# Modulation matmuls four units at a time in four column strips, and a wait moved to the evacuation of v

## What is computed

```python
mod = silu(c) @ w_ada + b_ada          # (9, 6*1024): 8 sample sequences and the prompt
shift1, scale1, gate1, shift2, scale2, gate2 = split(mod)
h = rmsnorm(x) * (1 + scale1) + shift1
q, k, v, conv..., gates... = h @ w_in  # w_in is (1024, 5120)
s = q @ k.T * HEAD_DIM ** -0.5 + rel_bias[:, rel]   # relative bias, then softmax, @ v
# then convolution, mixing, x += gate1 * mix, norm 2, routing, 32 experts, final norm
```

## Time and profile before

| | us |
|---|---|
| median of 3 runs | 1923.19 (1922.13 to 1927.28) |
| span of the profiled execution | 1918.4 |
| TensorE busy | 1676.0 (87%) |
| VectorE busy | 962.2 (50%) |
| ScalarE busy | 766.2 (40%) |
| POOL busy | 216.4 (11%) |

### The profile page before, as it was taken

The page is one execution under the profiler, slowest core; times in us unless marked ns, Lnnn a source line. Parts: engine busy times, 40 slices in busy tenths (PEclk is TensorE's granted clock), DMA queues, the critical chain, the costliest instruction groups (busy, mean ns, idle before and its releaser), DMA issues.

```text
span 1918.4 us, 22477 instructions
## 1 busy us (share of the span) xinstructions
PE 1676.0 (87%) x8467; PEld 1388.9 (72%) x8467; DVE 962.2 (50%) x1156; ACT 766.2 (40%) x869; POOL 216.4 (11%) x336
## 2 busy tenths in 40 slices
PE   6984999999989989999998994499999999999930
PEld 1244987886449989999997883377777777777720
DVE  0451102554320272222223545488888888888847
ACT  0221123663112022111121322077777777777734
POOL 2004401110000000000000002100000000000036
PEclk9997999999999999999998997699999999999965
DMA  9857512003421111211225333299999999999963
GB/s 344 284 84 219 191 64 71 1 2 113 157 68 54 44 34 31 83 50 50 58 71 199 121 99 110 92 398 398 396 396 395 395 394 394 396 391 393 342 220 142
DMA packets 194747, 371.34 MB, mean 194 GB/s; under 512 B 10699, under 2 KB 69107, under 8 KB 194546
## 3 DMA queue, kind: packets, MB, share of 16 engines
q1 hardware_dynamic: 170784, 289.92, 42.1%
q0 software_dynamic: 18976, 62.93, 10.2%
q10 hardware_dynamic: 4914, 17.49, 2.3%
HBM read 324.49 MB, written 47.89 MB: 194 GB/s over the span
## 4 chain that ended last, share of the span: by engine, by line
PE 74%; DVE 10%; ACT 6%; issue 3%; DMA 2%; another core or an unknown queue 2%; ACTq 1%; POOL 0%; SPq 0%; POOLq 0%; DVEq 0%; PEldq 0%
PE ps L1565 19%; PE ps L1567 18%; PE ps L1566 18%; PE ps L1548 4%; DVE mlo L1084 4%; ACT mhi L938 3%; PE ps L1692 3%; PE ps L1673 2%; ACT yy L958 2%; PE ps L1755 2%; PE ps L1732 2%; PE ps L1879 2%; PE ps L1682 1%; DMA bada<-in_b_ada_dram 1%
## 5 line engine op out<-in xcount | busy, mean ns | idle before, releaser
L1084 DVE TENSOR_TENSOR mlo<-mraw,mhi 128x2048 fp32r<-128x2048 f32 x188 | 420.5, 2288 | 38.9 <-ACT mhi L938 38.7
L938 ACT CAST mhi<-mraw 128x2048 fp32r<-128x2048 f32 x192 | 357.2, 1910 | 27.3 <-DMA mraw<-in_w_e_down_dram 27.2
L1565 PE MATMUL ps<-hTh,ring_r 128*128 128x384 f32 x864 | 291.2, 337 | 39.5 <-DVE ring_r L1084 31.6
L1567 PE MATMUL ps<-hTh,ring_r 128*128 128x384 f32 x864 | 290.6, 336 | 0.0
L1566 PE MATMUL ps<-hTl,ring_r 128*128 128x384 f32 x864 | 290.6, 336 | 0.0
L1565 PE MATMUL ps<-mhi,xTh 128*128 128x512 f32 x512 | 207.5, 405 | 22.0 <-DVE mlo L1084 19.6
L1566 PE MATMUL ps<-mlo,xTh 128*128 128x512 f32 x512 | 201.7, 394 | 0.0
L1567 PE MATMUL ps<-mhi,xTl 128*128 128x512 f32 x512 | 201.5, 394 | 0.0
L1565 PEld LDWEIGHTS ps<-hTh,ring_r 128*128 128x128 f32 x864 | 163.8, 190 | 41.2 <-DVE ring_r L1084 29.8
L1084 DVE TENSOR_TENSOR ring_r<-ring_f,ring_r 128x1024 fp32r<-128x1024 f32 x56 | 68.2, 1224 | 199.9 <-ACT ring_r L748 199.5
L1567 PEld LDWEIGHTS ps<-hTh,ring_r 128*128 128x128 f32 x864 | 163.6, 189 | 0.0
(11 more groups left out here) (302 smaller groups left out, 2549.4 us busy)
## 6 DMA issues: line engine op xcount, KB each, us to landing
mraw<-in_w_e_gate_dram SPq DMA_DIRECT2D x64, 1024.0 KB
mraw<-in_w_e_up_dram SPq DMA_DIRECT2D x64, 1024.0 KB
mraw<-in_w_e_down_dram SPq DMA_DIRECT2D x64, 1024.0 KB, 7.9
aring<-in_w_ada_dram SPq DMA_DIRECT2D x24, 1024.0 KB
ring_f<-in_w_in_dram SPq DMA_DIRECT2D x80, 256.0 KB, 4.5
y_d<-yy ACTq DMA_DIRECT2D x32, 512.0 KB, 6.8
y_d<-zrow POOLq DMA_DIRECT2D x68, 128.0 KB, 4.0
kc<-in_cache_attn_k_dram SPq DMA_DIRECT2D x8, 1024.0 KB, 5.3
```

The costliest lines, as they stand in the source:

```text
L938: nc.scalar.copy(mhi[j][:], mraw[j][:]).then_inc(s["gu_hi" if j < 4 else "d_hi"], 1)
L1084: V.tensor_tensor(out, value, high.bitcast(F32), ALU.subtract).then_inc(sig, 1)
L1565: mm(out, xh, wh, start=start, stop=False)
L1567: return mm(out, xl, wh, start=False, stop=stop)
```

## The change

The 12 units become three groups of four. `modulations(a)` runs the matmuls of a group slice by slice, the four units in turn; unit g of a group has its result in PSUM partitions 32g to 32g + 8 of one bank, so each uses its own strip of 32 columns of the array. `modc`, `bada` and `spread` get the same four strips of partitions. The ring for `w_ada` gets eight places: group 0 lies where `hTh` and `hTl` come later, groups 1 and 2 share the four old places. SP issues groups 0 and 1 at the start and group 2 when `unit_used` is 8. On TensorE group 0 comes first, then four spreads, group 1 ahead of the transposes of tile 3, group 2 after norm 1. The first six `w_in` units all wait for `unit_used` 12, and the first two chunks of q leave norm 1 and stand in `project` with the third. ScalarE's wait for `rel_out` moves to before the evacuation of v, its waits for `mod_out` go away, and POOL builds `spread` in four strips.

```diff
--- before.py
+++ after.py
@@ -164,7 +164,8 @@
 
-        aring = [at(f"aring{j}", [P, KT, 512], RING + j * SLOT if j < 3 else A(108)) for j in range(4)]
+        aring = [[at(f"aring{b}{j}", [P, KT, 512], A(16 * j) if b == 0 else RING + j * SLOT if j < 3 else A(108))
+                  for j in range(4)] for b in range(2)]
         hTh = at("hTh", [P, KT, T], A(0), F32R)
...
@@ -318,6 +319,9 @@
 
+        def ada_in(a, g):
+            return s["ada_mid"] if a == 1 else landed[g]
+
 
@@ -329,6 +333,11 @@
         NADA = 6 * D // 512
+        AG = NADA // 4
+
+        def strip(g):
+            return slice(32 * g, 32 * g + SEQS + 1)
+
         ada_units = [cols(w_ada2, c, 512) for c in range(NADA)]
...
@@ -397,22 +403,26 @@
 
-            for u, halves in enumerate(ada_units):
-                wait(sp, s["unit_used"], u - 3)
-                for i, src in enumerate(halves):
-                    sp.dma_start(aring[u % 4][:, 4 * i:4 * i + 4, :], src).then_inc(landed[u % 4], 16)
-                wait(sp, s["mod_sb"], u - 2)
-                sp.dma_start(bada[:, u % 3, :],
-                             bass.AP(b_ada.tensor, b_ada.offset + u * 512, [[0, SEQS + 1], [1, 512]])
-                             ).then_inc(landed[u % 4], 16)
+            for a in range(AG):
+                if a == 2:
+                    sp.wait_ge(s["unit_used"], 8)
+                for g in range(4):
+                    u = 4 * a + g
+                    sp.dma_start(bada[strip(g), a, :],
+                                 bass.AP(b_ada.tensor, b_ada.offset + u * 512, [[0, SEQS + 1], [1, 512]])
+                                 ).then_inc(ada_in(a, g), 16)
+                for i in range(2):
+                    for g in range(4):
+                        sp.dma_start(aring[min(a, 1)][g][:, 4 * i:4 * i + 4, :], ada_units[4 * a + g][i]
+                                     ).then_inc(ada_in(a, g), 16)
+
             def mixture(t):
                 wait(sp, s["o_done"], t - 1)
                 sp.dma_start(mix_parts(t)[1], mix_d[t]).then_inc(s[f"mix_in{t % 2}"], 16)
 
             for u, halves in enumerate(units):
                 if u == UK + 2:
-                    for r in range(3):
-                        sp.wait_ge(s[f"mod_out{r}"], MOD_OUT[r])
+                    sp.wait_ge(s["mod_out"], 16 * (NADA - 4))
                     sp.dma_start(modrep_d.rearrange("(q t) c -> q t c", t=DEC),
@@ -427,7 +437,7 @@
                 if u < NSLOT:
-                    sp.wait_ge(s["unit_used"], min(9 + u, NADA))
+                    sp.wait_ge(s["unit_used"], NADA)
                 elif u < NU - 2:
@@ -522,13 +532,15 @@
             link(nc.gpsimd.memset(spread[:], 1.0))
-            link(nc.gpsimd.affine_select(out=spread[:, 0, :], in_=spread[:, 0, :], compare_op=ALU.is_ge, fill=0.0,
-                                         base=-SEQROW, pattern=[[0, P]], channel_multiplier=1))
-            link(nc.gpsimd.affine_select(out=spread[:, 1, :], in_=spread[:, 1, :], compare_op=ALU.is_ge, fill=0.0,
-                                         base=0, pattern=[[1, P]], channel_multiplier=-DEC))
-            nc.gpsimd.affine_select(out=spread[:, 1, :], in_=spread[:, 1, :], compare_op=ALU.is_ge, fill=0.0,
-                                    base=DEC - 1, pattern=[[-1, P]], channel_multiplier=DEC
-                                    ).then_inc(s["consts"], 1)
+            for g in range(4):
+                own = spread[strip(g)]
+                link(nc.gpsimd.affine_select(out=own[:, 0, :], in_=own[:, 0, :], compare_op=ALU.is_ge, fill=0.0,
+                                             base=-SEQROW, pattern=[[0, P]], channel_multiplier=1))
+                link(nc.gpsimd.affine_select(out=own[:, 1, :], in_=own[:, 1, :], compare_op=ALU.is_ge, fill=0.0,
+                                             base=0, pattern=[[1, P]], channel_multiplier=-DEC))
+                link(nc.gpsimd.affine_select(out=own[:, 1, :], in_=own[:, 1, :], compare_op=ALU.is_ge, fill=0.0,
+                                             base=DEC - 1, pattern=[[-1, P]], channel_multiplier=DEC))
+            pool.sem_inc(s["consts"], 1)
             link(nc.gpsimd.memset(before[:], 1.0))
...
@@ -729,14 +740,13 @@
                 act.wait_ge(s["mod_sb"], u + 1)
-                act.dma_start(mod_d[:, u * 512:(u + 1) * 512], modc[:, u % 3, :]
-                              ).then_inc(s[f"mod_out{u % 3}"], 16)
+                act.dma_start(mod_d[:, u * 512:(u + 1) * 512], modc[strip(u % 4), u // 4, :]
+                              ).then_inc(s["mod_out"], 16)
 
             for u in range(2):
                 act.wait_ge(s["bc_ps"], u + 1)
                 for side in range(2):
                     nc.scalar.copy(shift1[:, side, u * 512:(u + 1) * 512], bank(6 + side)).then_inc(s["bc_sb"], 1)
-            modulation_out(4)
             act.wait_ge(s["consts"], 3)
@@ -765,18 +775,14 @@
                 b = 2 * (t % 2)
-                if t == 5:
-                    weights_high_to(1)
                 nc.scalar.copy(hTh[:, :, t * P:(t + 1) * P], bank(b, 2).rearrange("p (k c) -> p k c", k=KT)
                                ).then_inc(s["n1_evac"], 1)
-                if LEAD + t < NADA:
-                    modulation_out(LEAD + t)
+                if t in (4, 5, 6, 7):
+                    modulation_out(t)
 
             weights_high_to(2)
-            act.wait_ge(s["rel_out"], 16)
-
-            for r in range(3):
-                act.wait_ge(s[f"mod_out{r}"], MOD_OUT[r])
+            for u in range(8, NADA):
+                modulation_out(u)
             g = 0
@@ -799,6 +805,7 @@
                 g += 1
+            act.wait_ge(s["rel_out"], 16)
             for t in range(NT):
@@ -1048,12 +1055,9 @@
             def modulation(u):
-                dve.wait_ge(s["unit_used"], u + 1)
-                if u >= 7:
-                    dve.wait_ge(s[f"mod_out{u % 3}"], 16 * len(range(4 + (u - 4) % 3, u, 3)))
-                elif u >= 3:
-                    dve.wait_ge(s["bc_ps"], min(u - 2, 4))
-                V.tensor_tensor(modc[:, u % 3, :], ps[0:SEQS + 1, 4 + u % 2, :], bada[:, u % 3, :],
+                a, g = u // 4, u % 4
+                dve.wait_ge(s["unit_used"], 4 * a + 4)
+                V.tensor_tensor(modc[strip(g), a, :], ps[strip(g), 4 + a % 2, :], bada[strip(g), a, :],
                                 ALU.add).then_inc(s["mod_sb"], 1)
@@ -1065,9 +1069,6 @@
             V.tensor_copy(relrow[:, 4 * P:], bass.AP(relin, n, [[NREL, H], [-1, n]])).then_inc(s["rel_sb"], 1)
-
-            modulation(4)
-
 
@@ -1104,13 +1105,13 @@
                 V.tensor_tensor(ht[:, r, :], ht[:, r, :], shift1[:, side, :], ALU.add).then_inc(s["n1_h"], 1)
-                if LEAD + t < NADA:
-                    modulation(LEAD + t)
+                if t in (4, 5, 6, 7):
+                    modulation(t)
                 if t >= 1:
                     rows_rest(t - 1)
-                if t == 6:
-                    weights_rest_to(1)
             rows_rest(NT - 1)
+            for u in range(8, NADA):
+                modulation(u)
 
@@ -1541,13 +1542,15 @@
 
-            def modulation(u):
-                pe.wait_ge(landed[u % 4], 48 * (u // 4 + 1))
-                wait(pe, s["mod_sb"], u - 1)
+            def modulations(a):
+                wait(pe, s["mod_sb"], 4 * (a - 1))
+                for g in range(4):
+                    pe.wait_ge(ada_in(a, g), (48, 4 * 48, 96)[a])
                 for k in range(KT):
-                    last = mm(ps[0:n, 4 + u % 2, :], cT[:, k, :], aring[u % 4][:, k, :],
-                              start=(k == 0), stop=(k == KT - 1))
-                last.then_inc(s["unit_used"], 1)
+                    for g in range(4):
+                        last = mm(ps[strip(g), 4 + a % 2, :], cT[:, k, :], aring[min(a, 1)][g][:, k, :],
+                                  start=(k == 0), stop=(k == KT - 1))
+                last.then_inc(s["unit_used"], 4)
 
@@ -1592,8 +1595,7 @@
                         done += len(parts(c0, cn)) if split else 1
-                        if u0 > 0 or m > 0 or c == len(TOKCH) - 1:
-                            chunk_of(u0 + m, c, owner, base_count + done)
+                        chunk_of(u0 + m, c, owner, base_count + done)
                         if c0 == 0:
@@ -1606,27 +1608,23 @@
                 for side in range(2):
-                    last = mm(ps[:, 6 + side, :], spread[:, side, :], modc[:, u % 3, :], start=True, stop=True)
+                    last = mm(ps[:, 6 + side, :], spread[strip(u), side, :], modc[strip(u), 0, :],
+                              start=True, stop=True)
                 last.then_inc(s["bc_ps"], 1)
 
-            for u in range(LEAD + 1):
-                modulation(u)
-                if 1 <= u <= 4:
-                    spread_rows(u - 1)
+            modulations(0)
+            for u in range(4):
+                spread_rows(u)
             for t in range(NT):
                 r = t % 2
```

(25 more changed lines are left out.)

## The result

The changed kernel took 1945.95 us (median of four runs, 1945.16 to 1947.43), the kernel before 1924.38 (four runs, 1922.13 to 1927.28). The ratio is 1.0126, 95% interval 1.0112 to 1.0139. The medians lie 21.6 us apart, the ratio makes it 24. Forecast were 1941 and "slower". The profiled execution spans 1945.8 us, 27.4 more than the one of before (1918.4).

The account below looks back on a forecast made before the run. Loads sharing eight DMA engines with the bias table were taken to hold TensorE before 192 us. Group 2, weights and q's units put unit 1's end at 200.6, 17.6 later: 1918.4 to 1936.0, plus 4.8, about 1941; range 1932 to 1985.

Parts of the forecast that it names:

- Who held the hole of before: TensorE's 33 us wait near 133 us: weight unit 1's late landing beside the bias table's DMA, not the `rel_out` semaphore.
- One packet per turn on eight engines: DMA queues: eight engines serve one weight packet per table packet of 0.94 us, 64 turns for the table.
- Strips at 0.43 us per four: Modulation matmuls: four strips run together, so a group takes 6.9 us, plus 1.6 after idleness.
- Group 0: First four modulation units: data lands at about 34.5 us, matmuls run from 34.7 to 43.2.
- Spread and scale: Between group 0 and norm 1: 12.7 us from 43.2, with hops ending at 56.7; 7 us gained for norm 1.
- Norm 1, group 1, group 2, weights: Norm 1 3.8 us per tile; group 1 67.1 to 75.6; group 2 159.6 to 168.1; weights' first matmul at 174.
- Unit 0 of q: All three chunks now follow group 2 and take 14.1 us, to 188.1; unit 1 adds 12.5, to 200.6.
- Sum: q's unit 1 ends at 200.6 instead of 183.0, 17.6 us later; profiled span 1936.0, median 1940.8, say 1941.
- By parts: Summary of the loss: data 16 us later, unit 0 12.5 later, the stall as long as before.
- The moved wait: ScalarE's wait for `rel_out`, moved from before q to before v, never ended last, so gives nothing.
- Strips without overlap: Rival (a): a group's matmuls run serially, 27.5 us (cold 29.1); +60.7 us, about 1984; chance 0.18.
- a group 2 that passes the table: Rival (b), the second: engines serve many 2 KB packets per table packet, group 2 lands at 100 to 101; about 1881; chance 0.07.

Follow-up runs that it names:

- the wait-only run: Kernel before with one edit, ScalarE's wait for `rel_out` moved from ahead of q's evacuation to ahead of v's: 1921.03 us beside 1921.69, ratio 0.9999.
- the two-step table: Kernel before with the bias table written once to HBM, then from there to its 128 copies, 128 outermost: 1891.78 us, ratio 0.9844.
- fillers: Changed kernel with useless matmuls added, 115 ahead of group 0 and 5 after each of the first three spreads: 1948.73 us, ratio 1.0150.

## Why the prediction was right, and where it was short

- *Who held the hole of before.* Right: the wait-only run and the two-step table show it from both sides.
- *One packet per turn on eight engines.* Right for 2 KB packets too, 163 to 162, and 8 to 8 in one microsecond. Group 2 needed 82 us from issue to landing; 84 were forecast (75.7 to 159.5).
- *Strips at 0.43 us per four.* Right: groups of 7.9 to 9.8 us, 7.1 to 10.0 over all runs in this order. 64 matmuls of 0.43 are 27.5 one after another and took 7.09 at full clock, a gain of 3.9. The Trainium skill ("TensorE: Matmul & The Clock Gate", Measured speedup vs the span model) gives 2.38 for three strips; the 3.17 that an estimate by it makes of four is less than was measured. The 4 us kept for it weren't needed.
- *Group 0.* Forecast 34.7 to 43.2, was 36.5 to 46.4: landing 1.8 late, slow start 1.3 longer.
- *Spread and scale.* This is the term that was mis-sized. Three spreads of 3.76 for 1.95 make 5.4 us; norm 1 began at 66.0 and not at 56.7, the table went out at 84.4 and not at 74.5, and since everything behind hangs on the table's start, the 9.3 us went to the end. The prediction had "+4" for cold spreads in its range, not in its sum; its evidence was a spread at full clock that had a unit of 7 us ahead of it.
- *Norm 1, group 1, group 2, weights.* Each within 1 us of its length. Unit 0 of q took 15.3 for 14.1, the slow clock again.
- *Sum.* End of unit 1: forecast 200.6, was 211.2. Of the 10.6, 9.3 stem from ahead of norm 1 and 1.2 from unit 0. By the profiles the change costs 27.4 (17.6 forecast), by the runs 22 to 24. That 1941 came within 5 us of 1945.95 is in part luck: the prediction added 4.8 us to get from the span of before to its median. That profiled execution was a quick one, and that of the changed kernel was the slowest of its four. Span against span, 1936.0 was 9.8 short of 1945.8.
- *By parts.* The prediction's summary does not fit its own terms: it has the data 16 us later and the stall as long as before. Its steps have the first matmul after the stall 5.2 us later (174 for 168.84), which with the 12.5 makes the 17.7, and TensorE idle from 97 to 159.5, twice as long as before. The steps were right (60.5 us idle), the summary was not.
- *The moved wait.* Right: nothing.
- *Rivals.* Strips without overlap and a group 2 that passes the table are both out: 64 matmuls in 8 to 10 us, 163 packets to 162. The Trainium skill ("DMA: Bandwidth & Descriptors", Queues, rings and completion order) has an engine work off several descriptors before it turns to another queue; the records here turn after each. If both queues were served in batches alike, neither would pass the other, so the second rival, many packets of one for one of the other, doesn't follow from that rule either.

## What to carry over

Before speeding up what computes on loaded data, see on which engines its loads will run and what will run beside them: in this case a slow transfer from eight partitions took up eight DMA engines for its whole 66 us, and each load beside it paid one turn per packet. Count such a neighbour in turns, not in bytes; see how long its packets are on the queue it will use, and what else stands behind it there. And where work is packed tighter, small pieces that used to stand between long blocks stand alone: take their time at the low clock as well (here 3.76 us for 1.95).

## What the hardware showed besides

- Four fp32 matmuls of 9 columns, in four column strips, run wholly beside each other: 64 in 7.09 us at full clock, against 24 us when neighbours share a strip.
- The same 3 MB table took 65.7 us from 8 partitions on 8 engines; in two steps through HBM with 128 outermost it is off the path of the kernel before, which gains 30 us.
- The clock fell to 0.50 and stayed there for 14 us in which TensorE was busy for 97% with spreads and fillers.
- The same table came as 6.1 KB packets of 0.94 us from POOL's queue and as 3.05 KB packets of 0.46 us from ScalarE's, in the same 62 us or so.
- A small DMA issued behind the table on the same queue kept its engine 17.7 us in the issue, and VectorE waited 28.9 us for such DMAs to land.
